# The gate branch of a recurrent block: Gelu from the bank with tokens on partitions, then transposed

## The reference, cut to what matters

```python
proj = h @ w_in
gate = jax.nn.gelu(proj[..., :RG_WIDTH])
xc = causal_depthwise_conv(proj[..., RG_WIDTH:], conv_w, conv_b)
...
r = jax.nn.sigmoid(jnp.einsum('bshi,hij->bshj', xh, w_a).reshape(B, S, RG_WIDTH) + b_a)
i = jax.nn.sigmoid(jnp.einsum('bshi,hij->bshj', xh, w_x).reshape(B, S, RG_WIDTH) + b_x)
log_a = (-RG_C * r.astype(jnp.float32)) * jax.nn.softplus(-lam.astype(jnp.float32))
a = jnp.exp(log_a)
mult = jnp.sqrt(-jnp.expm1(2.0 * log_a))
bterm = mult * (i * xc).astype(jnp.float32)
_, hs = lax.associative_scan(lru_combine, (a, bterm), axis=1)
y = hs.astype(h.dtype) * gate
return y @ w_o
```

## Time and profile before

| | us |
|---|---|
| three runs | 1636.26, 1636.50, 1640.53 (median 1636.50) |
| the profiled execution | 1639.05 |
| its span, first to last instruction | 1637.3 |
| PE busy in the span | 1374.6 (84%) |
| DVE busy | 1066.9 (65%) |
| ACT busy | 561.9 (34%) |
| POOL busy | 532.7 (33%) |
| mean granted clock of PE, as a share of full speed | 0.934 |

### The profile page before, as it was taken

The page is one execution under the profiler, slowest core; times in us unless marked ns, Lnnn a source line. Parts: engine busy times, 40 slices in busy tenths (PEclk is TensorE's granted clock), DMA queues, the critical chain, the costliest instruction groups (busy, mean ns, idle before and its releaser), DMA issues.

```text
span 1637.3 us, 22696 instructions
## 1 busy us (share of the span) xinstructions
PE 1374.6 (84%) x8206; PEld 987.0 (60%) x8206; DVE 1066.9 (65%) x2068; ACT 561.9 (34%) x1048; POOL 532.7 (33%) x620
## 2 busy tenths in 40 slices
PE   8989999997999999999999548777767748776776
PEld 8979998896998888788888413233222213222222
DVE  5656765488776568877767957557765757557444
ACT  6656654466664454222441121211111211112111
POOL 8200010000000000000003656766576666666664
PEclk9999999998999999999999869987898969898888
DMA  8445565544565553311456989999899999999997
GB/s 254 148 131 155 180 202 197 180 130 145 168 204 190 186 175 103 104 51 58 152 169 242 398 308 371 382 356 363 330 410 352 358 358 378 372 361 358 351 365 294
DMA packets 184018, 408.96 MB, mean 250 GB/s; under 512 B 10674, under 2 KB 91868, under 8 KB 183916
## 3 DMA queue, kind: packets, MB, share of 16 engines
q0 software_dynamic: 74096, 269.52, 42.6%
q1 hardware_dynamic: 109516, 137.06, 25.8%
q10 hardware_dynamic: 304, 1.05, 0.2%
HBM read 406.54 MB, written 1.05 MB: 249 GB/s over the span
## 4 chain that ended last, share of the span: by engine, by line
PE 50%; issue 18%; DVE 13%; another core or an unknown queue 11%; POOL 4%; ACT 3%; DMA 1%; DVEq 0%; POOLq 0%; ACTq 0%
PE banks L2206 11%; PE banks L2207 11%; PE banks L2208 11%; PE banks L2680 3%; PE banks L2445 3%; DVE arena L2055 3%; POOL arena L913 2%; PE banks L2717 1%; PE banks L2542 1%; PE banks L2436 1%; POOL wring L913 1%; DVE h_raw L1660 1%; PE banks L2155 1%; POOL h_raw L913 1%
## 5 line engine op out<-in xcount | busy, mean ns | idle before, releaser
L913 POOL DMA_INDIRECT arena<-in_expert_u_dram,eidx x117 | 110.6, 945 | 703.2 <-DVEq L2035 643.0
L1412 DVE TENSOR_TENSOR w_a_low<-wring,w_a_high 128x1024 fp32r<-128x1024 f32 x192 | 235.8, 1231 | 127.6 <-ACT w_a_high L957 122.8
L2717 PE MATMUL banks<-arena 128*128 128x512 f32 x416 | 209.7, 648 | 92.7 <-issue 50.6
L1376 ACT ACTIVATE arena<-ident,arena 128x128 f32<-128x128 f32 x238 | 83.7, 394 | 494.5 <-issue 226.0
L957 ACT ACTIVATE w_a_high<-wring 128x1024 fp32r<-128x1024 f32 x192 | 201.3, 1052 | 131.2 <-PE banks L2208 128.7
L2206 PE MATMUL banks<-h_high,w_a_high 128*128 128x256 f32 (+1 forms) x832 | 238.0, 286 | 0.9 <-DVE h_low L1434 0.6
L2207 PE MATMUL banks<-h_low,w_a_high 128*128 128x256 f32 (+1 forms) x832 | 235.1, 283 | 0.0
L2208 PE MATMUL banks<-h_high,w_a_low 128*128 128x256 f32 (+1 forms) x832 | 233.5, 281 | 0.0
L2717 PEld LDWEIGHTS banks<-arena 128*128 128x128 f32 x416 | 80.8, 204 | 218.1 <-issue 174.6
L2717 PE MATMUL banks<-wring,arena 128*128 128x512 f32 x308 | 157.3, 654 | 50.8 <-issue 28.4
L2055 DVE CUSTOM_DVE_ANT_0 arena<-arena,banks 128x1024 f32<-128x1024 f32 x117 | 142.8, 1221 | 57.3 <-remote 20.6
(11 more groups left out here) (399 smaller groups left out, 2355.5 us busy)
## 6 DMA issues: line engine op xcount, KB each, us to landing
wring<-in_mlp_w_dram SPq DMA_DIRECT2D x64, 1024.0 KB, 5.4
wring<-in_w_in_dram SPq DMA_DIRECT2D x19, 1024.0 KB, 5.6
wring<-in_sb_w_qkv_dram SPq DMA_DIRECT2D x11, 1024.0 KB, 7.4
wring<-in_rg_w_in_dram SPq DMA_DIRECT2D x8, 1024.0 KB, 5.2
wring<-in_w_q_dram SPq DMA_DIRECT2D x8, 1024.0 KB, 5.4
wring<-in_sb_w_o_dram SPq DMA_DIRECT2D x4, 1024.0 KB, 5.3
wring<-in_rg_w_o_dram SPq DMA_DIRECT2D x4, 1024.0 KB, 5.0
wring<-in_w_o_dram SPq DMA_DIRECT2D x4, 1024.0 KB, 7.5
```

The costliest lines, as they stand in the source:

```text
L913: g.indirect_dma_start(out=grow(j), out_offset=None, in_=(expert_u, expert_v)[which][0], in_offset=bass.IndirectOffsetOnAxis(ap=eidx[:, tt ...
L1376: a.activation(diag[:, n % DIAGS, :], ident[:], ACT.Copy, scale=coef[:, tt, c0 + r:c0 + r + 1]).then_inc(diag_ready, 1)
L1412: v.tensor_tensor(unit(n, 1), raw_unit(n), unit(n, 0).bitcast(F32), ALU.subtract).then_inc(w_split, 1)
L2717: last = mm(y_banks[tt][half][:, :], diag[:, n % DIAGS, :], grow(j)[:, 512 * half:512 * (half + 1)], start=False, stop=True, skip_group_ch ...
```

## The change

The gate's half of `w_in` is now loaded and split as a phase in the second layout, `rg_gate`, with 8 units in place of rg8 to rg15. Its four banks (two halves of channels, two tiles of tokens) are read by ACT itself: Gelu with the token's factor as a scale per partition, 512 columns each, into SBUF with tokens on partitions. PE then transposes the result in four groups G0 to G3 (4 blocks of 128 x 128 each, with one group of key transposes behind each) and DVE multiplies each out of its bank by the scan, 512 columns at a time; ACT and DVE make the high and low parts per quarter. The key banks move from 0 to 3 to 7, 0, 3 and 6, the last two input-side products of `gate_inputs` lie inside the first half of `rg_gate`, and one unit's split on each engine moves behind the Gelu or the gated product.

```diff
@@ make_plan
-    for name, b in (("rg8", 0), ("ri6", 7), ("rg9", 1), ("ri7", 6)):
-        plan.add(name, b)
-    for m in range(KT + 2, 2 * KT):
-        plan.add(f"rg{m}", m - KT)
-    for m in range(4):
-        plan.add(f"key{m}", m)
+    for half in range(2):
+        for u in range(KT // 2 - 1):
+            plan.mark(f"rg_gate{half}_u{u}")
+            if half == 0 and u < 2:
+                plan.add(f"ri{KT - 2 + u}", 1 + u)
+        for tt in range(2):
+            plan.add(f"rg_gate{half}_{tt}", ACROSS["rg_gate"][2][2 * half + tt])
+    for half in range(2):
+        for j in (2 * half, 2 * half + 1):
+            plan.add(f"G{j}", (5, 6, 1, 2)[j])
+            plan.add(f"key{j}", (7, 0, 3, 6)[j])
...
+          "wo2": (5, KT, (0, 1, 2, 3), (4, 5, 6, 7)), "rg_gate": (0, KT, (7, 0, 3, 4), ())}
...
-        gate = area(8192, KT, SEQ)
+        gate = area(8192, 2, D)
+        gy = iS
@@ SP
-            for j in range(8):
-                c0 = (D if j < 4 else 0) + 256 * (j % 4)
-                load(SLOTS["rg_in"] + j, rg_w_in[0].rearrange("(k p) n -> p k n", p=P)[:, :, c0:c0 + 256], KT, 256)
+            load_columns("rg_in", rg_w_in[0], D, 4)
+            load_across("rg_gate", rg_w_in[0])
@@ ACT
                 a.activation(tS[:, h4], tS[:, h4], ACT.Ln, bias=1.0).then_inc(at_ready, 1)
-                split_high()
+                if m == 0:
+                    split_high()
...
-            for m in range(KT):
-                act.wait_ge(gate_in, m + 1)
-                a.activation(gate[:, m, :], gate[:, m, :], ACT.Gelu_apprx_tanh).then_inc(gelu_done, 1)
+            for half in range(2):
+                for tt in range(2):
+                    pb = wait_group(act, f"rg_gate{half}_{tt}")
+                    a.activation(gate[:, tt, 512 * half:512 * (half + 1)], pb[:, :], ACT.Gelu_apprx_tanh,
+                                 scale=rr[:, 4 + tt:5 + tt]).then_inc(free(f"rg_gate{half}_{tt}"), 1)
             split_high()
-            for m in range(2):
-                act.wait_ge(y_ready, m + 1)
-                h4 = slice(4 * m, 4 * m + 4)
-                a.activation(m_hl[0][:, h4, :], gate[:, h4, :], ACT.Copy).then_inc(gate_high, 1)
+            for j in range(KT // 2):
+                act.wait_ge(y_ready, j + 1)
+                a.activation(m_hl[0][:, 2 * j:2 * j + 2, :], gy[:, 2 * j:2 * j + 2, :], ACT.Copy).then_inc(gate_high, 1)
+            split_high()
             split_high(2)
@@ DVE
-            gate_input(0, 3)
...
                 dve.sem_inc(m_ready, 1)
-                gate_input(3 + m, 4 + m)
-                split_low()
+                if m == 0:
+                    split_low()
...
                 link(v.tensor_tensor(iS[:, h4], iS[:, h4], mS[:, h4], ALU.mult))
-                gate_input(5 + m, 6 + 2 * m)
...
+            def gated(j):
+                pb = wait_group(dve, f"G{j}")
+                two = slice(2 * j, 2 * j + 2)
+                v.tensor_tensor(gy[:, two, :], pb[:, :].rearrange("p (k n) -> p k n", n=SEQ), rS[:, two, :],
+                                ALU.mult).then_inc(y_ready, 1)
+            def gated_low(j):
+                dve.wait_ge(y_ready, j + 1)
+                dve.sem_inc(free(f"G{j}"), 1)
+                two = slice(2 * j, 2 * j + 2)
+                dve.wait_ge(gate_high, j + 1)
+                v.tensor_tensor(m_hl[1][:, two, :], gy[:, two, :], m_hl[0][:, two, :].bitcast(F32),
+                                ALU.subtract).then_inc(y_split, 1)
+            gated(0)
+            gated(1)
+            split_low()
+            gated_low(0)
+            gated(2)
+            gated_low(1)
+            gated(3)
+            gated_low(2)
+            gated_low(3)
+            split_low()
             for m in range(4):
                 pb = wait_group(dve, f"key{m}")
                 v.tensor_copy(keyT[:, 4 * m:4 * m + 4, :].rearrange("p a n -> p (a n)"),
                               pb[:, :]).then_inc(free(f"key{m}"), 1)
+                if m < 2:
+                    split_low()
@@ PE
-            for m in range(2, 2 * KT):
+            for m in range(2, KT):
                 project([f"rg{m}"], "rg_in", h_real, first=m)
-                if m < KT + 2:
-                    gate_inputs(m - 2)
+                gate_inputs(m - 2)
+            for half in range(2):
+                pbs = [open_bank(f"rg_gate{half}_{tt}") for tt in range(2)]
+                for u in range(KT // 2):
+                    w = split_unit(UNIT["rg_gate"] + KT // 2 * half + u)
+                    for tt in range(2):
+                        for kt in (2 * u, 2 * u + 1):
+                            last = products(pbs[tt][:, :], [t[:, kt, META + tt * P:META + (tt + 1) * P] for t in h_hl],
+                                            [t[:, kt - 2 * u, :] for t in w], kt == 0, kt == KT - 1)
+                        if tt or u == KT // 2 - 1:
+                            last.then_inc(group_done, 1)
+                    if half == 0 and u < 2:
+                        gate_inputs(KT - 2 + u)
             pe.wait_ge(keys_loaded, 16)
-            for m in range(4):
...
-            across("rg_o", m_hl, lambda kt: (y_split, kt // 4 + 1))
+            for half in range(2):
+                wait_out(pe, *[f"rg_gate{half}_{tt}" for tt in range(2)])
+                for m in (2 * half, 2 * half + 1):
+                    pb = open_bank(f"G{m}")
+                    for kt in (2 * m, 2 * m + 1):
+                        for tt in range(2):
+                            c0 = SEQ * (kt % 2) + tt * P
+                            last = transposed(pb[:, c0:c0 + P], gate[:, tt, kt * P:(kt + 1) * P], P)
+                    last.then_inc(group_done, 1)
+                    pb = open_bank(f"key{m}")
+                    for j in range(4):
+                        last = transposed(pb[:, j * P:(j + 1) * P], keyT[:, 4 * m + j, :], P)
+                    last.then_inc(group_done, 1)
+            across("rg_o", m_hl, lambda kt: (y_split, kt // 2 + 1))
```

More of the change, by code:

```diff
@@ L358 @@
 _at = 0
-for _name, _count in (("qkv", 12), ("wo", 4), ("up0", 16), ("down0", 16), ("rg_in", 8), ("rg_o", 4),
+for _name, _count in (("qkv", 12), ("wo", 4), ("up0", 16), ("down0", 16), ("rg_in", 4), ("rg_gate", 4), ("rg_o", 4),
                       ("up1", 16), ("down1", 16), ("w_conv", 4), ("w_rwkv", 7), ("w_gate", 8),
@@ L373 @@
           "rg_o": (3, KT, (4, 5, 6, 7), (0, 1, 2, 3)), "down1": (4, FF // P, (0, 1, 2, 3), (4, 5, 6, 7)),
-          "wo2": (5, KT, (0, 1, 2, 3), (4, 5, 6, 7))}
+          "wo2": (5, KT, (0, 1, 2, 3), (4, 5, 6, 7)), "rg_gate": (0, KT, (7, 0, 3, 4), ())}
 CROSSED_BY = {b: name for name, (b, _, _, _) in ACROSS.items()}
@@ L404, in make_used_at @@
         of(name, *[f"{name}{half}_{f'u{u}' if u < last else 1}" for half in range(2) for u in range(last + 1)])
-    of("rg_in", *[f"rg{m}" for m in range(2 * KT)])
+    of("rg_in", *[f"rg{m}" for m in range(KT)])
     of("w_conv", *[f"{n}{m}" for n in ("val", "cg") for m in range(RT)])
@@ L626, in build @@
             "h_whole", "h_high", "w_high", "w_split", "gate_high", "y_high", "y_split", "mix_high"))
-        gate_in, gelu_done = sem("gate_in"), sem("gelu_done")
         mix_split, meta_ready, meta_high, meta_split = map(sem, (
@@ L1584, in _, with input_gate @@
             dve.wait_ge(rs_ready, RS_AT[2])
[L1586 to L1592, removed]
+            def input_gate(m):
+                wait_out(dve, f"ri{m}")
+                mark(v.scalar_tensor_tensor(iS[:, m, :], iS[:, m, :], 2.0 ** 0.5, xc[:, m, :], ALU.mult, ALU.mult))
             for m in range(KT):
@@ L1604, in _ @@
             for m in range(KT):
-                wait_out(dve, f"ri{m}")
-                mark(v.scalar_tensor_tensor(iS[:, m, :], iS[:, m, :], 2.0 ** 0.5, xc[:, m, :], ALU.mult, ALU.mult))
+                input_gate(m)
                 if m >= 5:
@@ L1625, in _ @@
                 settle()
[L1626 to L1632, removed]
-                                ALU.subtract).then_inc(y_split, 1)
-            split_low(3)
+            def gated(j):
[9 more added lines that the diff above has]
+                v.tensor_tensor(m_hl[1][:, two, :], gy[:, two, :], m_hl[0][:, two, :].bitcast(F32),
+                                ALU.subtract).then_inc(y_split, 1)
+            gated(0)
[8 more added lines that the diff above has]
+            split_low()
             for m in range(4):
@@ L2410, in _ @@
             spread("rb2", 4)
-            for m in range(2, 2 * KT):
+            for m in range(2, KT):
                 project([f"rg{m}"], "rg_in", h_real, first=m)
-                if m < KT + 2:
-                    gate_inputs(m - 2)
-            pe.wait_ge(keys_loaded, 16)
-            for m in range(4):
-                pb = open_bank(f"key{m}")
-                for j in range(4):
-                    last = transposed(pb[:, j * P:(j + 1) * P], keyT[:, 4 * m + j, :], P)
-                last.then_inc(group_done, 1)
-            across("rg_o", m_hl, lambda kt: (y_split, kt // 4 + 1))
```

(9 more changed lines are left out.)

## The result

Before: 1634.88 us, median of 22 runs (1628.68 to 1640.53). After: 1639.80 us, median of 22 (1634.72 to 1645.31). The ratio is 1.0027, 95% interval [1.0017, 1.0037]: the changed kernel is about 4.4 us slower, where 3.7 us less were forecast. The profiled execution of after took 1642.84 us, with a span of 1641.1.

What follows compares the result with a forecast made beforehand. PE was taken as the bound (busy 84%), with an 8.77 us hole before `rg_o`. 5.3 us won at full clock, less the low clock's cost, gave -3.7 us: 1636.5 to 1632.8 us, range 1630.5 to 1635.3.

Steps and rivals of the forecast that it cites:

- PE's gate phase: Gate matmuls on PE: fewer, wider steps of 0.227 us save 0.8 us, ending near 378.3 instead of 379.15.
- Scans: DVE's scans, without the eight gate inputs between them, end at 381.4 instead of 386.1: 4.7 us won.
- ACT's table load and G0's start: Before the transposes: ACT's table load (1.28 us) begins at 377.7, PE begins G0 at 380.25.
- The Gelu: ACT's four Gelus of 512 columns, read from a bank, take 0.56 us each.
- The slower rival: ACT's four Gelus delay the joint: slower from 1.6 us each; at 2.9 us each, 1641.7 us. Chance 0.04.
- The first matmul of `rg_o`: PE starts `rg_o` at about 385.5 against 389.83, with key3 waiting for DVE's third gated product.
- The clock: Transposes before `rg_o` don't hold PE's clock; its first unit runs ten slow steps, cutting the gain to 3.7 us.
- the first rival: The clock holds through the transposes before `rg_o`: gain 5.3 us, set by unit 17's split, 1631.2 us. Chance 0.27.
- the wait for unit 17: The second unit of `rg_o` waits for unit 17's split until 389.2; before, it began at 394.51.
- Behind the joint: After `rg_o`'s start, everything later waits on PE, so the 3.7 us gain carries to the end undiminished.

Runs made afterwards that it cites:

- after_2: The changed kernel run once more unaltered, for a second trace; PE stops at the same instruction as in the first trace, for 3.60 us.
- pad40: The changed kernel with 40 tiny fp32 matmuls (160 instructions) on four tiles in turn in front of G0; 1631.63 us, ratio 0.9966 to the kernel before.
- pad20: The changed kernel with 20 tiny fp32 matmuls (80 instructions) on four tiles in turn in front of G0; 1634.3 us, ratio 0.9988 to the kernel before.
- late_load: The changed kernel with one second-block 1 MB `w_gate` load held back until PE finished the loop of small matmuls; 1555.44 us, ratio 0.9983 to the kernel before.
- pad40_2: The run pad40 once more, on a chip where the kernel before takes 1558.49 us; 1554.08 us, ratio 0.9966 to the kernel before.
- before_pad24: The kernel before with 24 tiny fp32 matmuls (96 instructions) in PE's long hole in front of `rg_o`; 1643.57 us, ratio 1.0041 to the kernel before.
- before_2: The kernel before run once more unaltered, for a second trace; its joint took 80.90 us.
- before_pad48: The kernel before with 48 tiny fp32 matmuls (192 instructions) in PE's idle time in front of `rg_o`; 1637.92 us, ratio 1.0010 to the kernel before.

## Why the prediction was wrong

**PE's gate phase: close.** Forecast end 378.3, with the shift 381.6; PE ended at 381.81 + 0.23 = 382.0, so half of the 0.8 us was won. The steps are 0.23 us. PE waits behind it either way.

**Scans: right.** Forecast 381.4, shifted 384.7; measured 382.17 + 2.44 = 384.6. ACT's table load and G0's start (383.71, forecast 383.5) fit to 0.2 us.

**The Gelu: close.** The four start 0.58 us apart, against 0.56 taken. The slower rival needed 1.6 each.

**The first matmul of `rg_o`: 1 us early.** I had key3 wait until DVE was done with its third gated product (gated 2), with the start at 388.8 when shifted. The 32 transposes never paused, though that product started only at 387.59, after the last of them had ended. The release of G1's bank is an instruction of its own, written behind that product, and the trace has it at 386.14, ahead of the product: DVE issued it while earlier work was still queued. The first matmul waited for the low part instead (0.42). Nothing came of it, since unit 17's split decides next.

**The clock: wrong.** This is the first step that failed. I took it that transposes don't keep the clock up and gave the fall the larger chance. In all six traces of the changed kernel in which little stands between the gate's last matmul and the transposes (after, `after_2`, `pad40`, `pad20`, `late_load`, `pad40_2`) the clock stayed at 1.00 and the joint took 74.93 to 74.97 us; in all four of the old joint it fell (80.08 to 80.90). The program's start, which I had for evidence, showed a clock that had not risen; it says little on one that is up. The rule of the Trainium skill that I weighed (page "TensorE: Matmul & The Clock Gate", section "Part 4: PE-mode transpose") is not borne out here: 3.7 us of transposes behind 1.5 us of idle time left the clock high. The stretch without a large matmul was not too short for a fall: it is 5.8 us in after (382.0 to 387.8), and in before the clock fell at 383.6, 4.5 us behind the gate's last large matmul, with 1.9 us of transposes in between the earlier trace rows. No run took the transposes alone away, so that it is they that hold the clock is argued from these traces, not tested. The joint's gain was the first rival's 5.3 us, with the wait for unit 17 in the place that it named (392.40, forecast 389.2 + 3.3 = 392.5).

**Behind the joint: wrong, and this decided.** "Everything later waits on PE [...] so I carry the gain to the end undiminished." The gain did arrive, undiminished, at 612 us. The step that failed is the term behind the joint, put at nothing: what was missing is a cost of the change that no edited line shows, 164 instructions fewer on PE. The rows to see it were there before (the instruction queue's 60 packets on the page, and the change's 80 matmuls fewer: eight groups of 24 and 16 transposes are 208, 96 and 32 are 128), but I looked only at what the instructions do. With the code put back in place the kernel is at 0.9966, 5.6 us under before, as rival 1 had it; the interval is 3.3 to 7.9 us, so that the two differ by only 0.3 is partly luck. The price of the place is then 1.0027 - 0.9966, some 10 us; measured on the old kernel (`before_pad24`) it is 6.7. The intervals of the two overlap.

**What stays open.** How the 9 us between 612 and 810 divide. To 694 it is +5.57: the hole of 3.88, and a fall of the clock at 676.2, ahead of the hole, that before doesn't have. `before_2` has such a fall (at 679.5) without the hole, and its stretch is 83.81 us against 82.37 in before, so that fall is worth some 1.4 us and is no work of the change. From 694 it is +3.32: the holes of 1.09 and 1.58 (before has 0.51 and 0.34 in this stretch), and the clock at 0.50 from 696.7 to 700.1, right behind the hole of 3.88. The fall is there behind all three holes of 3.6 to 3.9 us at this place and not behind the one of 1.18, but no run has the long hole without it. The attention's +3 us in both traces of after goes with falls of the clock at 109.6 and 116.4 us. The pads stand behind that stretch, so PE's code in front of it is the same in `pad40`, which had only the first fall and 130.53 us; I put it to chance. The medians leave little room for it: the stretch's 8.9 us less the joint's 5.3 are 3.6, and the ratio gives 4.4 (2.8 to 6.0). What holds a packet back when the DMA engines are idle was not tried.

## What to carry to other kernels

An edit that changes the number of an engine's instructions moves the fetches of everything behind it. In a kernel tuned to under a percent, compare the holes without a releaser ("issue") of both traces, and measure the change once more with the count padded back before judging it; here this turned 0.27% slower into 0.34% faster. If such a hole lies beside a large load, hold the load back or move the code: here 80 instructions (`pad20`) were enough to take the hole from 3.88 to 1.47 us.

## What the hardware did that was not expected

- PE stops without a releaser only at instruction counts that are multiples of 256 apart, and goes on 2.2 to 2.8 us behind the start of an instruction packet (all eleven traces, 640 to 740 us).
- PE runs dry for 1.2 us at a fixed instruction when the DMA engines are idle, and for 3.6 to 3.9 us when a 1 MB weight load is ahead of the fetch (`late_load`, after, `after_2`, `before_pad24`).
- 32 transposes (3.68 us) between idle pieces of 1.5 and 0.4 us keep the clock at 1.00; 160 matmuls of 32 x 32 on one tile (6.02 us) directly behind the gate's large ones let it fall to 0.50 within about 4 us of their start.
- The same small matmuls cost 3.22 / 96 = 0.034 us each on one tile of the array (`before_pad48`, clock at 1.00), and 0.89 / 80 = 0.011 us on four tiles in turn (`pad40`).
